# Modulations on four column groups: a two-block transformer kernel on one Trainium2 core

## The reference, cut to what matters

```python
silu_c = jax.nn.silu(c)[:, None, :]
silu_cc = jax.nn.silu(c_ctx)[None, None, :]
for i in range(DEPTH):        # two layers
    sh1, sc1, gt1, sh2, sc2, gt2 = jnp.split(silu_c @ ada_w[i] + ada_b[i], 6, axis=-1)
    csh1, csc1, cgt1, csh2, csc2, cgt2 = jnp.split(silu_cc @ ada_w[i] + ada_b[i], 6, axis=-1)
    h = rmsnorm(x, norm1_g[i]) * (1.0 + sc1) + sh1
    ...
```

## Time and profile before

| | |
|---|---|
| median of 3 runs | 4038.93 us (4038.79 to 4040.79) |
| profiled execution, first to last instruction | 4033.4 us |
| TensorE busy | 3659.4 us, 91% |
| VectorE busy | 2076.6 us, 51% |
| ScalarE busy | 1534.6 us, 38% |
| mean granted TensorE clock | 0.953 |
| DMA | 378.48 MB, mean 94 GB/s |

### The profile page before, as it was taken

How to read it: one execution, slowest core, us unless ns; L and a number is a source line. 1 busy time by engine, 2 the same in 40 slices (tenths; PEclk the granted TensorE clock), 3 DMA queues, 4 the chain that set the end, 5 groups by cost and what they waited for, 6 DMA issues and landing times.

```text
span 4033.4 us, 59667 instructions
## 1 busy us (share of the span) xinstructions
PE 3659.4 (91%) x24596; PEld 2835.1 (70%) x24596; DVE 2076.6 (51%) x3393; ACT 1534.6 (38%) x2762; POOL 230.5 (6%) x447
## 2 busy tenths in 40 slices
PE   7889999999977886889889999979999999799998
PEld 4744577778865565788758887756788666568886
DVE  3365443333457563566454445664544545544445
ACT  4466542222234562233253333442433434443334
POOL 0011000000000011333230000000000000000000
PEclk9999999999998887899999999988999999899999
DMA  4111123322212555566522222111222221012221
GB/s 183 38 63 63 63 74 115 115 105 84 74 66 85 156 143 152 150 157 164 135 90 84 105 94 104 66 41 59 73 94 105 73 81 53 32 68 96 93 95 62
DMA packets 294205, 378.48 MB, mean 94 GB/s; under 512 B 240432, under 2 KB 243376, under 8 KB 259248
## 3 DMA queue, kind: packets, MB, share of 16 engines
q1 hardware_dynamic: 280560, 328.78, 25.3%
q10 hardware_dynamic: 13376, 45.87, 3.0%
HBM read 330.56 MB, written 44.06 MB: 93 GB/s over the span
## 4 chain that ended last, share of the span: by engine, by line
PE 75%; DVE 10%; ACT 6%; DMA 3%; issue 3%; POOL 2%; SPq 1%; ACTq 0%; DVEq 0%; POOLq 0%
PE ps L256 18%; PE ps L257 17%; PE ps L258 17%; PE ps L336 3%; PE ps L772 2%; PE ps L1267 1%; PE ps L1269 1%; PE ps L1268 1%; DMA s_it<-rt 1%; DVE mx L1567 1%; PE ps L762 1%; DVE wlo L248 1%; ACT whi L241 1%; POOL ri L2214 1%; POOL tp L2211 1%
## 5 line engine op out<-in xcount | busy, mean ns | idle before, releaser
L248 DVE TENSOR_TENSOR wlo<-panel,whi 128x512 fp32r<-128x512 f32 (+1 forms) x519 | 498.3, 961 | 347.4 <-ACT whi L241 338.7
L241 ACT ACTIVATE whi<-panel 128x512 fp32r<-128x512 f32 (+1 forms) x519 | 437.0, 842 | 580.3 <-PE ps L258 579.0
L256 PE MATMUL ps<-dh,whi 128*128 128x512 f32 (+1 forms) x1280 | 474.9, 371 | 0.0
L257 PE MATMUL ps<-dh,wlo 128*128 128x512 f32 (+1 forms) x1280 | 472.7, 369 | 0.0
L258 PE MATMUL ps<-dl,whi 128*128 128x512 f32 (+1 forms) x1280 | 470.9, 368 | 0.0
L256 PE MATMUL ps<-xh,whi 128*128 128x512 f32 x1088 | 443.5, 408 | 27.9 <-DVE xl L2529 22.2
L257 PE MATMUL ps<-xh,wlo 128*128 128x512 f32 x1088 | 430.2, 395 | 0.0
L258 PE MATMUL ps<-xl,whi 128*128 128x512 f32 x1088 | 428.3, 394 | 0.0
L256 PE MATMUL ps<-hh,whi 128*128 128x512 f32 (+1 forms) x960 | 352.8, 368 | 26.6 <-DVE hl L456 26.4
L257 PE MATMUL ps<-hh,wlo 128*128 128x512 f32 (+1 forms) x960 | 340.3, 355 | 0.0
L258 PE MATMUL ps<-hl,whi 128*128 128x512 f32 (+1 forms) x960 | 339.7, 354 | 0.0
(11 more groups left out here) (536 smaller groups left out, 6066.1 us busy)
## 6 DMA issues: line engine op xcount, KB each, us to landing
panel<-in_w SPq DMA_DIRECT2D x248, 1024.0 KB, 4.8
late<-s_fe ACTq DMA_DIRECT2D x16, 1024.0 KB, 6.9
late<-s_fe ACTq DMA_DIRECT2D x48, 256.0 KB, 5.3
s_fe<-x SPq DMA_DIRECT2D x37, 256.0 KB, 2.7
late<-s_fe ACTq DMA_DIRECT2D x8, 768.0 KB, 6.6
s_fe<-x SPq DMA_DIRECT2D x40, 128.0 KB, 2.7
s_ia<-panel SPq DMA_DIRECT2D x24, 128.0 KB, 3.0
s_ia<-gg SPq DMA_DIRECT2D x24, 128.0 KB, 2.7
```

The costliest lines, as they stand in the source:

```text
L241: e.activation(unit(u)[0][:, 0:kc, :], w, ACT.Copy).then_inc(*w_hi.up(u))
L248: e.tensor_tensor(lo[:, 0:kc, :], w, hi[:, 0:kc, :].bitcast(F32), SUB).then_inc(*w_lo.up(u))
L256: e.matmul(out, hi[:, k, :], xh, start=k == 0, stop=False)
L257: e.matmul(out, lo[:, k, :], xh, start=False, stop=False)
```

## The change

A unit's eight products no longer go all to rows 0 and 1 of the bank. Product k goes to the 32 array columns and the 32 PSUM partitions of group k mod 4, so each group adds up two of the eight. For that the weights are read 32 columns wide, from column 2k on; the silu tile gets 30 more columns, set to zero, so that the last reads stay inside it. Of the 32 rows of a group only the first two are wanted. `ada_row` copies all 128 partitions, `AROW` is 128 x 256, and the turn becomes an ordinary fp32 product: the 128 x 128 half of `AROW` is the weight, and a 128 x 2 matrix `sel`, with a 1 where the partition modulo 32 equals the column, is the moving operand. It adds the four partial sums and turns them in one.

```diff
@@ allocation
-    SC = alloc(ctx, [P, 8, 2], name="silu")
-    SM = alloc(ctx, [P, 64], name="small")
-    AROW = [alloc(ctx, [2, 256], name="arow") for _ in range(2)]
+    SCW = alloc(ctx, [P, 46], name="silu")
+    SC = SCW[:, 0:16].rearrange("p (k c) -> p k c", c=2)
+    SM = alloc(ctx, [P, 16], name="small")
+    AROW = [alloc(ctx, [P, 256], name="arow") for _ in range(2)]
@@ start_dve, start_pe
+        e.memset(SCW[:, 16:46], 0.0).then_inc(*sc_dv.up("zero"))
...
         e.wait_ge(*sc_dv.at("silu"))
+        e.wait_ge(*v_in.at("vec"))
@@ ada_mm
-        row = ada_bank(n)[0:2, 0:256]
...
-            i = e.matmul(row, SC[:, k, :], w[:, k * 256:k * 256 + 256], start=k == 0, stop=k == 7)
+            j = k % 4
+            i = e.matmul(ada_bank(n)[32 * j:32 * j + 32, 0:256], SCW[:, 2 * k:2 * k + 32], w[:, k * 256:k * 256 + 256],
+                         start=k < 4, stop=k > 3)
@@ ada_tr
-        e.transpose(out[:, 0:2], AROW[n % 2][:, 0:P], ID[0:2, 0:2])
-        e.transpose(out[:, 2:4], AROW[n % 2][:, P:2 * P], ID[0:2, 0:2]).then_inc(*ad_tr.up(n))
+        e.matmul(out[:, 0:2], AROW[n % 2][:, 0:P], vec("sel", 0, 2), start=True, stop=True)
+        e.matmul(out[:, 2:4], AROW[n % 2][:, P:2 * P], vec("sel", 0, 2), start=True, stop=True).then_inc(*ad_tr.up(n))
@@ ada_row
-        e.activation(AROW[n % 2][:, :], ada_bank(n)[0:2, 0:256], ACT.Copy).then_inc(*ad_ac.up(n))
+        e.activation(AROW[n % 2][:, :], ada_bank(n)[:, 0:256], ACT.Copy).then_inc(*ad_ac.up(n))
@@ host side
+    put("sel", (np.arange(P)[:, None] % 32 == np.arange(2)[None, :]).astype(f))
```

More of the change, by code:

```diff
@@ L38, in _vec_layout @@
                     ("subg", 1), ("hgg", 1), ("lb", 8), ("lam", 4), ("e6", 1), ("e5", 1), ("egn", 1),
-                    ("l10", 1)]:
+                    ("l10", 1), ("sel", 2)]:
         VCOLS[name] = (at, n)
@@ L296, in start_act @@
         e.wait_ge(*v_in.at("vec"))
-        e.activation(SC[:, :, :], vec("c", 0, 16).rearrange("p (k c) -> p k c", c=2), ACT.Exp,
+        e.activation(SC, vec("c", 0, 16).rearrange("p (k c) -> p k c", c=2), ACT.Exp,
                      scale=-1.0).then_inc(*sc_ac.up("exp"))
     def start_dve(e):
+        e.memset(SCW[:, 16:46], 0.0).then_inc(*sc_dv.up("zero"))
         e.wait_ge(*c_in.at("cst"))
@@ L303, in start_dve @@
         e.wait_ge(*sc_ac.at("exp"))
-        e.tensor_scalar(SC[:, :, :], SC[:, :, :], 1.0, None, ADD).then_inc(*sc_dv.up("one"))
+        e.tensor_scalar(SC, SC, 1.0, None, ADD).then_inc(*sc_dv.up("one"))
         e.wait_ge(*sc_dv.at("one"))
-        e.reciprocal(SC[:, :, :], SC[:, :, :]).then_inc(*sc_dv.up("rec"))
+        e.reciprocal(SC, SC).then_inc(*sc_dv.up("rec"))
         e.wait_ge(*sc_dv.at("rec"))
-        e.tensor_tensor(SC[:, :, :], SC[:, :, :], vec("c", 0, 16).rearrange("p (k c) -> p k c", c=2),
+        e.tensor_tensor(SC, SC, vec("c", 0, 16).rearrange("p (k c) -> p k c", c=2),
                         MUL).then_inc(*sc_dv.up("silu"))
```

## The result

The changed kernel takes **3983.61 us** (median of 4 runs, 3975.15 to 3984.26), the kernel before in the same measurement 4039.86 us (4 runs, 4038.79 to 4045.57): a ratio of 0.9861, interval 0.9846 to 0.9877, so 56 us or 1.4% faster. The forecast was 3978, its range 3960 to 3998.

The account below looks back on a forecast made before the run. TensorE was taken as the bound, busy 91% of the span. MLP 59 + start 8 - attention 6 = 61 us off the span of 4033.4 gave 3972, plus 5.5 from span to median 3978; range 3960 to 3998.

Parts of the forecast that it names:

- clock rival: Attention: the clock falls behind nearly every unit, 24 instead of 8 us lost, 3994 us; 15%.
- The products in the MLP: First MLP, 24 units: four column groups overlap, 3.45 us becomes 0.90, saving 2.55 each, 61 us.
- the estimate of 3.2 times: MLP products: the skill's 2.38 times for three groups carried on to four; 1.09 us a unit, 57 instead of 61.
- 0.19 for getting in and out: MLP, around each unit's products: tiling-mode drain seems paid already; were it new, the sum would lose 5 us.
- The turn: MLP, L342 and L343: 0.4 instead of 0.30 us, a loss of 0.1 each, 2 us over 24 units.
- The start: Start stage: shorter units, limited by DMA and VectorE's sums; L450 at about 40.5 instead of 48.74, 8 us gained.
- The attention: Attention, 16 units: small gain where PE is last, outweighed by clock falls behind longer pauses; 6 us lost in sum.
- half of the 14 falling: Attention: the clock falls behind half of some 14 pauses, 1.2 us counted each; 8 us lost (bounds 0 and 24).
- 2 us of gain: Attention: 3.5 us gained where PE is last, less 1.5 for sixteen dearer turns.
- Two at a time: Products: only two groups overlap, a unit takes 1.94 us, MLP gains 34, 38 in all, 4001 us; 12%.
- no overlap: Products: groups don't overlap with 256 moving columns, turns alone cost 2 + 2 + 1 us, 4044 us; 5%.
- records that wait for each other's end: Products: records of different groups run singly, a unit takes 6.1 us, 63 more over the MLP, 4100 us; 3%.

Follow-up runs that it names:

- both: Changed kernel with the attention units of the kernel before, plus stand-in matmuls in pauses of the start stage: 3971.77 us, ratio 0.9847.
- att_old: Changed kernel with the sixteen attention units put back to the products, copy and turn of the kernel before: 3966.31 us, ratio 0.9832.
- att_x4: Changed kernel with each attention unit's short products issued four times over, new turns kept: 3977.26 us, ratio 0.9858.
- two_groups: Changed kernel with a unit's eight products sent to two groups of 32 columns, copy and turn of 64 rows: 3999.17 us (one run).
- pairs: Changed kernel with the two products of each group following each other directly in the program: 3978.73 us (one run).

## Why the prediction was right

Its mechanism held: the gain is made in the MLP, a little at the start, and part of it is lost in the attention to the clock. 3983.61 lies between the forecast of 3978 and the clock rival's 3994.

- **The products in the MLP, 2.55 us each.** Measured 2.55. All four groups overlap in full with 256 moving columns, as the earlier trace rows had shown with 64. The Trainium skill (TensorE: Matmul & The Clock Gate, "Measured speedup vs the span model") has 2.38 times for three groups; had the estimate of 3.2 times held that the prediction carried on from it, a unit's stream would be 1.09 us beside the 0.19 around it. It is 0.90, so the measured factor is 3.45 / 0.90 = 3.8. The 0.19 for getting in and out were there before and were not paid a second time.
- **The turn, 0.4 instead of 0.30.** Measured 0.37. The loads, the copy of 128 rows and the wider tables cost nothing that can be seen: the MLP's sum was 59, the stage shows 58.1.
- **The start, 8 us.** The step that failed here is the size of the term: 3.8. Panel 3 was forecast for 19.6 and came at 22.30, panel 4 for 24.6 and came at 25.83; and I took units after the first at full clock, where they took 1.94 us. L359 of unit 3 came at 28.75, not 26.7: 1.2 of the 2.05 us from the panel, 0.8 from the clock. L359 of unit 5 came at 37.42, not 34.2, another 1.2 us with unit 6 at half clock. The last 1.1 us come behind: the totals L416 take 2.91 us where L412 took 1.56, more than the 0.4 allowed for a lower clock. Units 6 and 7 and the totals at full clock, as the run both has them, give 3.1 us back, which confirms the clock's part; what held panel 3 back for 2.7 us no run shows. That the clock was low in the changed kernel too rests on its records' pace and on att_old, whose windows have the same pace at 0.50.
- **The attention, +6 us.** The step "with half of the 14 falling" was mis-sized: 11 more low stretches than before, not 7, two of them twice as long as the 3.2 us of the earlier trace rows. By att_old and att_x4 most of the loss belongs to the clock. With the 2 us of gain that I had counted, 15.3 us over 11 stretches are 1.4 each; I had 1.2. That the gain of 2 was there is not shown by itself.
- **The rivals.** The clock rival came about in number (11 of 14) but not in price (24 us expected, 15 found). Two at a time would have made units of 1.94 us, as two_groups in fact has, and did not occur with four groups; neither did no overlap, nor records that wait for each other's end. The rule of strict program order in the Trainium skill (TensorE: Matmul & The Clock Gate, "The mechanism") would make the order of pairs slow, since the 13th record could not run beside the first; the block is 1.09 us, so for products of different column groups these runs speak against it, and so does, as the prediction said.
- **Span and median.** The terms add up to 61, the span gave 51.2; of the 9.8 between, 4.2 are the start, 7.3 the attention, 0.9 the MLP, and 2.6 went the other way in stages that the change does not touch. That the forecast median is only 5.6 us off is partly chance. It carried the 5.5 us between span and median over from before; in every run on record the time lies only 1.8 to 1.9 us above that run's own span, so the rest was a profiled execution of before that ran faster than its median. With 1.9 the same terms give 3974. By the medians the gain is 56 us (50 to 62 by the interval), which holds both the 61 of the sum and the 51 of the spans.

What stays open: which pauses let the clock fall. The timeline of the changed kernel, 37 us before the place shown above:

```profile
276.91 1.90 PE L776 MATMUL ps<-pt,v 128*64 128x512 f32 x4 [2.81 <-ACT pt L818]
```

Here PE had waited 2.81 us for the copy, and its four products took 1.90 us, at full clock; at 313.88 it had waited 2.82 and they took 3.65. No run tells the two apart. What is shown is only that shorter pauses, of up to 2.0 us in two_groups, left four low stretches, and those of up to 3.0 us here thirteen.

## What to carry to other kernels

A product with few output columns, which leaves most of TensorE's columns idle, can be cut into four groups of 32 columns at almost four times the pace (0.90 us instead of 3.47 here, for products of 256 columns), if something as cheap as a product with a 0/1 matrix adds up the groups. Do it where TensorE sets the time, and leave it where TensorE would only wait: a shorter piece in front of a wait makes a pause, and here the pauses, with the low clock behind them, cost 14 us in a stage where the piece had cost next to nothing. The kernel with the change everywhere but in the attention, att_old, is the one to keep: 3966 us, 1.7% below before, though it is the attention of the profiles and not the times that sets it apart from the changed kernel.

## What was unexpected about the hardware

- More work made a stage faster: 41 us of repeated products in the attention took 9 us off it; the granted clock over the stage was 0.97 instead of 0.91.
- Two turns with 128 x 128 weights are cheaper in a stream of 128 x 128 products than two with 32 or 64 rows: 0.37 against 0.63 us. The smaller shape has a gap of nearly 0.1 us on either side, the full one none ahead of it.
- Products of different column groups overlapped in both orders tried, within 16 records.
- A window can read a granted clock of 1.00 while its records run at half pace, as in the first 45 us of the changed kernel, whose trace has no entry of the clock before 57.0 us; read the clock from a known record there too.
